# Moving the low part of weight sum S1 behind the next turn's first partial sum

## The chip, the cores and the metric

One core of a Trainium2 chip runs the kernel. The metric is device time in microseconds for one execution. TensorE multiplies matrices into PSUM, VectorE (DVE), ScalarE (ACT) and GpSimd (POOL) work on tiles, and SyncE (SP) issues most of the transfers.

## The reference

The kernel computes a two-layer encoder in fp32: 1024 features, 1280 tokens (1024 of one sequence, 256 of another). Each layer has a mixer of three kinds of heads and then a SwiGLU feed-forward part; the change is in the latter:

```
hf = rmsnorm(x, g_pre_ffn)
f = (jax.nn.silu(hf @ w_gate) * (hf @ w_up)) @ w_down
return x + rmsnorm(f, g_post_ffn)
```

`w_gate` and `w_up` have 2816 columns, which is 22 blocks of 128.

## The kernel before

Everything is written out by hand: one instruction list per engine, and semaphores between them. Each engine works through its own list in order.

**Splitting.** For fp32 accuracy each operand is split in a high part (ScalarE copies it to the fp32r type) and a low part (the operand minus its high part, formed by VectorE or GpSimd). A product is then made of high times high, high times low and low times high: three matmuls where there would be one.

**Turns.** Gate and up are computed together with a Strassen-like scheme: seven products instead of eight, over sums of weight blocks (S1 to S4) and sums of stream blocks (T1 to T4). One *turn* is the seven products for one block of 128 columns and one half of the tokens, in this order: A11, S2, A12, S3, S1, A22, S4. A product is 4 x 3 matmuls. A turn of token half 0 is wide (384 columns), one of half 1 narrow (256 columns). There are 44 turns per layer, numbered t = 0 to 43. A *visit* is one block of weights: visits 0 to 8 have one wide turn each (t = 0 to 8), visits 9 to 21 a wide and a narrow one (t = 9 to 34), visits 22 to 30 one narrow one (t = 35 to 43). Weights of the visits alternate between two buffers GR (raw), GH (high) and GL (low), numbered v % 2.

**Within a turn VectorE** forms six partial sums from PSUM (`partial`): u2 after product S2, u3 after S3, gate2 after S1, gate1 after A22, up2 and hid1 after S4. Product S3 reuses the PSUM bank of S2 and waits for u2; A22 waits for u3; S4 waits for gate2. Between them, in the first turn of a visit, VectorE prepares the next visit's weights: the sums S1 and S3 behind u2, S2 behind u3, S4 behind gate2 (`weight_sum`, one line of 128 x 512 each), and the low parts of S2, S3 and S1 (`weight_sum_low`). From visit 2 on, S1 is held in a PSUM bank of its own (`Y_BANK`), and the S1 sum of a visit waits until the S1 low part of the visit before it has been formed:

```
if v > 1:
    dve.wait_ge(s_wlo_v, 3 * VISIT[L, v] - 3)
```

**ScalarE** makes the high parts of the sums, in the order S1, raw (three blocks at once), S3, S2, S4. **GpSimd** waits for the raw high part and forms three raw low parts (A22, A11, A12, line 1265), then the S4 low part (1273), and then multiplies `hidden2` (1281), which waits for up2. In turns 8 and 9 it also forms low parts of the stream for token half 1 (line 1288: B11, B21, then T1, T4, B22), which products of turn 10 read first; VectorE forms T2 and T3 (line 2035) at the start and the end of turn 9. In turns 3 and 5 GpSimd has a `fold` (line 1244) ahead of its raw low parts.

**The last turns.** Behind turns 38, 40 and 42 VectorE forms the sum S3B (line 2109) and the low part DWL (line 2169) for the down product, and behind turns 39, 41 and 43 the low part DHL (line 2180).

Of the kernel before, what the change touches and what calls it, by code (L numbers as in the profile page):

```python
# [75 lines left out]
NV = len(VISITS)  # L76
TURNS = [(v, u, g) for v, (u, gs) in enumerate(VISITS) for g in gs]
# [375 lines left out]
def build(nc, xt, w_in, w_out, w_gu, w_down, gains, conv_w, rpb, tables, small, mixed,  # L453
          parked, hidden, out):
    with ExitStack() as ctx:
# [315 lines left out]
        def product_at(L, t, name):  # L771
            return NPR * (TURN[L, t] - 1) + PRODUCTS.index(name) + 1

        def turns_of(f):
            return [t for t, (_, u, _) in enumerate(TURNS) if u == f]

        def stored(L, t):
            return 32 * (NT // 2 * L + t // 2 + 1)
# [69 lines left out]
        def summed_weights(L, v, name):  # L848
            return 4 * (VISIT[L, v] - 1) + SUM_ORDER.index(name) + 1

        def high_weights(L, v, name):
            return 5 * (VISIT[L, v] - 1) + HIGH_ORDER[v].index(name) + 1

        def weight_sum_at(v, name):

            if name == "S1" and v > 1:
                return PS[:, Y_BANK, :].rearrange("p (t n) -> p t n", n=P)
            if name == "S2" and v >= EVENTS_OVER:
                return PS[:, SUM_BANK, :].rearrange("p (t n) -> p t n", n=P)
            return GR[v % 2][:, BLOCK[name], :, :]  # L860
# [4 lines left out]
        def bank(t, which):  # L865
            return 3 * (t % 2) + "abc".index(which)
# [1086 lines left out]
        def _(dve):  # L1953
# [63 lines left out]
            def mix(L, g, name):  # L2017

                key, C = (L, g, name), CF[g]
                if name == "T1":  # L2020
                    dve.wait_ge(s_xn, XNORM[L, 2 * g + 1, KT - 1])
                    if g == 0:
                        dve.wait_ge(s_group, GROUP[L, "o", 5, 3])
                else:
                    dve.wait_ge(s_mixsum, MIXSUM[key] - 1)
                out, a, b = {"T1": ("T1", "T3", "B11"), "T2": ("T2", "B22", "T1"), "T3": ("T3", "B22", "T3"),
                             "T4": ("T4", "B21", "T2")}[name]
                nc.vector.tensor_tensor(C[out][:, :, :], C[a][:, :, :], C[b][:, :, :], ALU.subtract) \
                    .then_inc(s_mixsum, MIXSUM.step(key))

            def combination_low(L, g, name):

                dve.wait_ge(s_chi, CHI[L, g, name])
                dve.wait_ge(s_mixsum, MIXSUM[L, g, AFTER[name]])
                nc.vector.tensor_tensor(CL[g][name][:, :, :], CF[g][name][:, :, :], CH[g][name][:, :, :].bitcast(F32),
                                        ALU.subtract).then_inc(s_clo_v, CLO_V.step((L, g, name)))
# [28 lines left out]
            def weight_sum_low(L, v, name):  # L2065

                m = BLOCK[name]
                dve.wait_ge(s_whi, high_weights(L, v, name))
                dve.wait_ge(s_wsum, summed_weights(L, v, "S4" if name == "S2" else "S2" if name == "S1" else "S3"))
                nc.vector.tensor_tensor(GL[v % 2][:, m, :, :], weight_sum_at(v, name),  # L2070
                                        GH[v % 2][:, m, :, :].bitcast(F32), ALU.subtract).then_inc(s_wlo_v, 1)

            def partial(L, t, what):

                n, key = widths[TURNS[t][2]], TURN[L, t]
                T1, U2, U3 = (tile[t % 2][:, 0:n] for tile in (S1T, U2T, U3T))
                a, b, c = (PS[:, bank(t, which), 0:n] for which in "abc")
                if what == "u2":
                    dve.wait_ge(s_product, product_at(L, t, "S2"))
                    dve.wait_ge(s_first, key)  # L2080
                    if key > 2:
                        dve.wait_ge(s_hout[t % 2], stored(L, t) - 32)
                    nc.vector.tensor_tensor(U2, b, T1, ALU.add).then_inc(s_u2, 1)  # L2083
                elif what == "u3":
                    dve.wait_ge(s_product, product_at(L, t, "S3"))
                    if key > 2:
                        dve.wait_ge(s_hid2, key - 2)
                    nc.vector.tensor_tensor(U3, b, T1, ALU.add).then_inc(s_u3, 1)
                elif what == "gate2":
                    dve.wait_ge(s_product, product_at(L, t, "S1"))  # L2090
                    dve.wait_ge(s_u3, key)
                    nc.vector.tensor_tensor(U3, c, U3, ALU.add).then_inc(s_gate2, 1)
                elif what == "gate1":
                    dve.wait_ge(s_product, product_at(L, t, "A22"))
                    nc.vector.tensor_tensor(T1, b, T1, ALU.add).then_inc(s_gate1, 1)
                elif what == "up2":
                    dve.wait_ge(s_product, product_at(L, t, "S4"))
                    dve.wait_ge(s_u2, key)
                    nc.vector.tensor_tensor(U2, c, U2, ALU.add).then_inc(s_up2, 1)
                else:  # L2100
                    dve.wait_ge(s_silu1, key)
                    nc.vector.tensor_tensor(T1, a, T1, ALU.mult).then_inc(s_hid1, 1)

            def sum_s3(L, p):

                n = AT_STEP["A11", p]
                dve.wait_ge(s_s3in, 16 * NPAIR * (L + 1))
                dve.wait_ge(s_ring_w[n % RING], ring_loads(L, n)[0])
                nc.vector.tensor_tensor(S3B[p][:, :, :], DWR[n % RING][:, :, :], S3B[p][:, :, :], ALU.subtract) \
                    .then_inc(s_s3, 1)  # L2110
# [331 lines left out]
            for L in range(DEPTH):  # L2442
# [97 lines left out]
                for t, (v, _, g) in enumerate(TURNS):  # L2540
                    prepare = (t == 0 or TURNS[t - 1][0] != v) and v + 1 < NV
                    partial(L, t, "u2")
                    if t == 0:
                        combination_low(L, 0, "T1")
                        combination_low(L, 0, "T4")
                    if t == 8:
                        mix(L, 1, "T4")
                        mix(L, 1, "T3")
                    if t == 9:
                        combination_low(L, 1, "T2")  # L2550
                    if prepare and v:
                        weight_sum(L, v + 1, "S1")
                        weight_sum(L, v + 1, "S3")
                    if 1 <= t < 5:
                        for k in range(2):
                            step(e, 2 + t // 3, 4 - 4 * (t % 2) + k)
                    if t in (5, 7):
                        for k in range(3) if t == 5 else range(5, KT):
                            normed(L, 2 + t // 7, k)
                    partial(L, t, "u3")  # L2560
                    if t == 0:
                        combination_low(L, 0, "B22")
                    if prepare and v:
                        weight_sum(L, v + 1, "S2")
                    partial(L, t, "gate2")
                    if prepare and v:
                        weight_sum(L, v + 1, "S4")
                    if prepare:
                        weight_sum_low(L, v + 1, "S2")
                    partial(L, t, "gate1")  # L2570
                    if prepare:
                        weight_sum_low(L, v + 1, "S3")
                        weight_sum_low(L, v + 1, "S1")
                    partial(L, t, "up2")
                    partial(L, t, "hid1")
                    if 1 <= t < 5:
                        for k in range(2, 4):
                            step(e, 2 + t // 3, 4 - 4 * (t % 2) + k)
                    if t in (5, 6):
                        for k in range(3, KT) if t == 5 else range(5):  # L2580
                            normed(L, t - 3, k)
                    if t == 7:
                        for name in MIX_ORDER[:2]:
                            mix(L, 1, name)
                    if t == 9:
                        combination_low(L, 1, "T3")
                    if t in EARLY_AT:
                        sum_s3(L, EARLY_AT.index(t))
                        down_low_weights(L, EARLY_AT.index(t))
                    if t - 1 in EARLY_AT:  # L2590
                        down_low_stream(L, EARLY_AT.index(t - 1))
# [539 lines left out]
```

## Time and profile before

| | us |
|---|---|
| median of 3 runs | 3009.96 (3009.44 to 3010.25) |
| the profiled execution, its own time | 3009.93 |
| its span in the profile | 3008.1 |
| TensorE busy | 2977.9 (99%) |
| VectorE busy | 2017.8 (67%) |
| ScalarE busy | 1240.6 (41%) |
| GpSimd busy | 928.9 (31%) |

A busy share is an average over all stages. TensorE's is so near to the span that other engines matter only where TensorE waits for them, so the places to look at are single gaps of tenths of a microsecond. Matmuls overlap in the profile (each is shown longer than the distance to the next), so a short gap shows in the distance between starts.

### The profile page before, as it was taken

What the parts mean: (1) busy time and instruction counts of PE and PEld (TensorE: products, weight loads), DVE (VectorE), ACT (ScalarE), POOL (GpSimd) and SP (SyncE); (2) the same over time, 40 slices, a digit from 0 to 9 for tenths busy, and PEclk for the clock granted to TensorE, in tenths of its full rate; (3) what the DMA queues carried; (4) which work ended last, traced back from release to release, by engine and by line L of the source; (5) the groups of instructions that cost most, each with busy time, mean ns of one, the idle gap of its engine ahead of it and who ended that gap; (6) DMA issues with size and microseconds to landing.
All of it is one profiled execution on the core that took longest, in us unless ns stands there. A gap on an engine that the chain in (4) does not pass through costs nothing.

```text
span 3008.1 us, 50968 instructions
## 1 busy us (share of the span) xinstructions
PE 2977.9 (99%) x19620; PEld 2819.5 (94%) x19620; DVE 2017.8 (67%) x3735; ACT 1240.6 (41%) x2401; POOL 928.9 (31%) x762
## 2 busy tenths in 40 slices
PE   9999999999999999999999999999999999999998
PEld 8888888999999999999988888889999999999998
DVE  7866766388744447677888667573886444486786
ACT  5433444544422225444554344444543222254342
POOL 1211111665532225101442111127555222360013
PEclk9999999999999999999999999999999999999999
DMA  4111011333222226644531110122332222257345
GB/s 157 45 58 52 22 39 57 116 106 110 95 69 72 69 70 198 211 140 152 180 108 47 50 57 20 41 66 100 120 116 93 71 69 69 81 177 253 98 141 197
DMA packets 151568, 300.32 MB, mean 100 GB/s; under 512 B 16288, under 2 KB 74272, under 8 KB 151072
## 3 DMA queue, kind: packets, MB, share of 16 engines
q1 hardware_dynamic: 148336, 288.00, 28.8%
q10 hardware_dynamic: 2992, 9.05, 0.8%
q8 instruction: 159, 2.61, 0.4%
q14 instruction: 81, 0.66, 0.1%
HBM read 231.45 MB, written 57.67 MB: 96 GB/s over the span
## 4 chain that ended last, share of the span: by engine, by line
PE 91%; DVE 4%; POOL 1%; issue 1%; ACT 1%; DMA 1%; SPq 0%; POOLq 0%; DVEq 0%; ACTq 0%
PE PS L2663 27%; PE PS L2665 26%; PE PS L2664 26%; PE PS L2784 4%; PE PS L2815 3%; PE PS L2799 3%; PE PS L2701 1%; POOL OSS L1237 1%; PE PS L2759 1%; DVE ACCUM L1986 0%; PE PS L2824 0%; DVE PT L2383 0%; DMA ACCUM<-xt 0%; DVE SW L2274 0%; DMA DHR<-hidden 0%
## 5 line engine op out<-in xcount | busy, mean ns | idle before, releaser
L2663 PE MATMUL PS<-XH,WH 128*128 128x512 f32 (+1 forms) x1152 | 432.0, 375 | 4.2 <-DVE XL L2230 1.7
L2665 PE MATMUL PS<-XH,WL 128*128 128x512 f32 (+1 forms) x1152 | 409.6, 356 | 0.0
L2664 PE MATMUL PS<-XL,WH 128*128 128x512 f32 (+1 forms) x1152 | 407.9, 354 | 0.0
L1265 POOL TENSOR_TENSOR GL<-GR,GH 128x512 fp32r<-128x512 f32 x186 | 251.8, 1365 | 366.5 <-ACT GH L1614 304.8
L2663 PE MATMUL PS<-DHH,DWH 128*128 128x384 f32 (+1 forms) x1056 | 328.5, 311 | 1.1 <-DVE ACCUM L2215 1.1
L2665 PE MATMUL PS<-DHH,DWL 128*128 128x384 f32 (+1 forms) x1056 | 326.6, 309 | 0.0
L2664 PE MATMUL PS<-DHL,DWH 128*128 128x384 f32 (+1 forms) x1056 | 325.9, 309 | 0.0
L2663 PEld LDWEIGHTS PS<-XH,WH 128*128 128x128 f32 x1152 | 217.2, 189 | 53.3 <-issue 17.7
L2665 PEld LDWEIGHTS PS<-XH,WL 128*128 128x128 f32 x1152 | 217.2, 189 | 32.9
L2664 PEld LDWEIGHTS PS<-XL,WH 128*128 128x128 f32 x1152 | 217.9, 189 | 24.6
L2664 PE MATMUL PS<-CL0T,GH 128*128 128x384 f32 x704 | 238.4, 339 | 0.0
L2663 PE MATMUL PS<-CH0T,GH 128*128 128x384 f32 x704 | 237.7, 338 | 0.0
L2665 PE MATMUL PS<-CH0T,GL 128*128 128x384 f32 x704 | 236.2, 335 | 0.0
L1571 ACT ACTIVATE PT<-PS 128x512 fp32r<-128x512 f32 (+1 forms) x328 | 142.8, 477 | 223.9 <-PE PS L2799 219.6
L1319 POOL COPY RC<-STAT 128x128 f32<-128x128 f32 x100 | 31.9, 319 | 633.6 <-DVE STAT L2392 633.3
L2663 PE MATMUL PS<-CH1T,GH 128*128 128x256 f32 x704 | 198.4, 282 | 2.7 <-DVE U2T L2083 2.7
L2663 PEld LDWEIGHTS PS<-DHH,DWH 128*128 128x128 f32 x1056 | 198.9, 188 | 1.5 <-DVE ACCUM L2215 1.3
L2665 PEld LDWEIGHTS PS<-DHH,DWL 128*128 128x128 f32 x1056 | 198.7, 188 | 0.0
L2664 PEld LDWEIGHTS PS<-DHL,DWH 128*128 128x128 f32 x1056 | 198.6, 188 | 0.0
L2665 PE MATMUL PS<-CH1T,GL 128*128 128x256 f32 x704 | 198.4, 282 | 0.0
L2664 PE MATMUL PS<-CL1T,GH 128*128 128x256 f32 x704 | 196.8, 279 | 0.0
L2383 DVE TENSOR_TENSOR PT<-PS,PT 128x512 fp32r<-128x512 f32 (+1 forms) x328 | 163.8, 531 | 32.5 <-ACT PT L1571 31.0
(242 smaller groups left out, 8341.3 us busy)
## 6 DMA issues: line engine op xcount, KB each, us to landing
GR<-w_gu SPq DMA_DIRECT2D x62, 768.0 KB, 4.2
RAW<-w_in SPq DMA_DIRECT2D x48, 512.0 KB, 3.5
DHR<-hidden SPq DMA_DIRECT2D x66, 320.0 KB, 4.7
DWR<-w_down SPq DMA_DIRECT2D x66, 256.0 KB, 4.0
S3B<-w_down SPq DMA_DIRECT2D x66, 256.0 KB, 3.3
GR<-w_gu SPq DMA_DIRECT2D x62, 256.0 KB, 2.5
T3B<-hidden SPq DMA_DIRECT2D x44, 320.0 KB, 4.0
hidden<-S1T SPq DMA_DIRECT2D x44, 192.0 KB, 1.9
```

The source lines that it names most:

```text
L1237: nc.gpsimd.tensor_tensor(into, into, pair_of(e, kind, c)[:, k % 2, 0:n], ALU.add) \
L1265: nc.gpsimd.tensor_tensor(GL[v % 2][:, m, :, :], GR[v % 2][:, m, :, :], GH[v % 2][:, m, :, :].bitcast(F32), ALU.subtract).then_inc(s_wlo_r ...
L1319: nc.gpsimd.tensor_copy(RC[:, :, :], SM[:, a:a + 2].unsqueeze(2).to_broadcast([P, 2, HD])) \
L1571: nc.scalar.activation(PT[u % 2][:, 0, a:a + n, :].rearrange("p t q -> p (t q)"), PS[:, 4 + g, 0:n * P], ACT.Copy).then_inc(s_pth, 1)
L2383: nc.vector.tensor_tensor(PT[u % 2][:, 1, a:a + n, :].rearrange("p t q -> p (t q)"), PS[:, 4 + g, 0:n * P], high.bitcast(F32), ALU.subtract) \
L2663: nc.tensor.matmul(out, wh, xh, start=first, stop=False, skip_group_check=reopened)
L2664: nc.tensor.matmul(out, wh, xl, start=False, stop=False, skip_group_check=reopened)
L2665: return nc.tensor.matmul(out, wl, xh, start=False, stop=last, skip_group_check=reopened)
L2701: last = nc.tensor.matmul(PS[:, at, j:j + 1], sq[:, j * P:(j + 1) * P], ones[:, 0:1], start=m == 0, stop=m == len(squares) - 1)
L2784: last = nc.tensor.matmul(PS[:, 2 * h + a // 4, 0:n * P], qs[own, :], k[own, keys], start=m == 0, stop=m == 2)
L2799: last = nc.tensor.transpose(PS[:, 4 + g, j * P:(j + 1) * P], PR[:, u % 2, (a + j) * P:(a + j + 1) * P], ident)
L2815: last = nc.tensor.matmul(PS[:, Y_BANK, 2 * P * h:2 * P * h + 2 * P], values_of(b, i, k0, a, h), PT[h][:, :, a, :], start=a == 0, stop=a = ...
```

## The change

In the list of VectorE the S1 low part of the next visit leaves its place behind the S3 low part, ahead of up2. It is formed in the following turn, right behind u2 and ahead of everything else in that turn. The wait of the S1 sum quoted above stays, and the instruction on which it waits now stands right in front of it where the next turn forms sums. No other engine's list changes.

```diff
                 for t, (v, _, g) in enumerate(TURNS):
                     prepare = (t == 0 or TURNS[t - 1][0] != v) and v + 1 < NV
                     partial(L, t, "u2")
+                    if t and (t == 1 or TURNS[t - 2][0] != TURNS[t - 1][0]) and TURNS[t - 1][0] + 1 < NV:
+                        weight_sum_low(L, TURNS[t - 1][0] + 1, "S1")
                     if t == 0:
                         combination_low(L, 0, "T1")
                         combination_low(L, 0, "T4")
...
                     partial(L, t, "gate1")
                     if prepare:
                         weight_sum_low(L, v + 1, "S3")
-                        weight_sum_low(L, v + 1, "S1")
                     partial(L, t, "up2")
                     partial(L, t, "hid1")
```

VectorE's list at the end of turn 40 and the start of turn 41, before. `GL<-GR,GH` is the S3 low part, `GL<-PS,GH` behind it the S1 low part, `U2T<-PS,U2T` up2, `S1T<-PS,S1T` hid1, `S3B` and `DWL` the early work of the down product, `U2T<-PS,S1T` u2 of turn 41 and `PS<-GR` the S1 sum.

```order
 L2070 TENSOR_TENSOR GL_203<-GR_205,GH_201 128x512
 L2070 TENSOR_TENSOR GL_203<-PS,GH_201 128x512
 L2099 TENSOR_TENSOR U2T_155<-PS,U2T_155 128x256
 L2102 TENSOR_TENSOR S1T_153<-PS,S1T_153 128x256
 L2109 TENSOR_TENSOR S3B_268<-DWR_218,S3B_268 128x512
 L2169 TENSOR_TENSOR DWL_213<-DWR_218,DWH_208 128x512
 L2083 TENSOR_TENSOR U2T_156<-PS,S1T_154 128x256
 L2063 TENSOR_TENSOR PS<-GR_206 128x512
```

The same place after the change.

```order
 L2070 TENSOR_TENSOR GL_203<-GR_205,GH_201 128x512
 L2099 TENSOR_TENSOR U2T_155<-PS,U2T_155 128x256
 L2102 TENSOR_TENSOR S1T_153<-PS,S1T_153 128x256
 L2109 TENSOR_TENSOR S3B_268<-DWR_218,S3B_268 128x512
 L2169 TENSOR_TENSOR DWL_213<-DWR_218,DWH_208 128x512
 L2083 TENSOR_TENSOR U2T_156<-PS,S1T_154 128x256
 L2070 TENSOR_TENSOR GL_203<-PS,GH_201 128x512
 L2063 TENSOR_TENSOR PS<-GR_206 128x512
```

The S1 low part has moved from ahead of up2 to between u2 and the S1 sum of the next turn.

VectorE's list at the start of turn 8, as a piece of the difference. `CF1T` are the mixes of the stream.

```order
 L2028 TENSOR_TENSOR CF1T_171<-CF1B_168,CF1T_170 128x1024
 L2083 TENSOR_TENSOR U2T_155<-PS,S1T_153 128x384
+L2070 TENSOR_TENSOR GL_203<-PS,GH_201 128x512
 L2028 TENSOR_TENSOR CF1T_172<-CF1B_167,CF1T_171 128x1024
 L2028 TENSOR_TENSOR CF1T_169<-CF1B_168,CF1T_169 128x1024
```

Here the low part stands ahead of two mixes, which are followed by the S1 sum of turn 8.

## Rows read from the trace of the kernel before

**Rows 1.** Both turn stretches summed (676:1216, 2167:2710): busy us of each engine.
```profile
sum 1083.00, PE 1080.33 PEld 1078.36 DVE 649.10 ACT 377.45 POOL 449.86; mean PE 540.16 PEld 539.18 DVE 324.55 ACT 188.72 POOL 224.93
```
**Rows 2.** Timeline, VectorE, turns 39 to 41: start, us, line, out<-in, idle before.
```profile
1182.78 1.35 DVE L2180 TENSOR_TENSOR DHL<-DHR,DHH 128x640 fp32r<-128x640 f32 x1
1184.06 0.41 DVE L2083 TENSOR_TENSOR U2T<-PS,S1T 128x256 f32<-128x256 f32 x1
1184.39 0.68 DVE L2063 TENSOR_TENSOR PS<-GR 128x512 f32<-128x512 f32 x1
...
1189.86 1.65 DVE L2070 TENSOR_TENSOR GL<-GR,GH 128x512 fp32r<-128x512 f32 x1
1191.43 0.68 DVE L2070 TENSOR_TENSOR GL<-PS,GH 128x512 fp32r<-128x512 f32 x1
...
1192.37 0.41 DVE L2102 TENSOR_TENSOR S1T<-PS,S1T 128x256 f32<-128x256 f32 x1
1192.70 1.22 DVE L2109 TENSOR_TENSOR S3B<-DWR,S3B 128x512 f32<-128x512 f32 x1
1194.02 0.69 DVE L2169 TENSOR_TENSOR DWL<-DWR,DWH 128x512 fp32r<-128x512 f32 x1
1194.63 0.42 DVE L2083 TENSOR_TENSOR U2T<-PS,S1T 128x256 f32<-128x256 f32 x1
```
**Rows 3.** Timeline, TensorE, end of product A12 and start of S3, turn 41.
```profile
1194.44 0.28 PE L2664 MATMUL PS<-CL1B,GH 128*128 128x256 f32 x1
1194.56 0.28 PE L2665 MATMUL PS<-CH1B,GL 128*128 128x256 f32 x1
1195.19 0.36 PE L2663 MATMUL PS<-CH1T,GH 128*128 128x256 f32 x1 [0.35 <-DVE U2T L2083]
```
**Rows 4.** Timeline, GpSimd, turn 40.
```profile
1187.16 3.80 POOL L1265 TENSOR_TENSOR GL<-GR,GH 128x512 fp32r<-128x512 f32 x3 [3.71 <-ACT GH L1614]
1190.92 1.75 POOL L1273 TENSOR_TENSOR GL<-GR,GH 128x512 fp32r<-128x512 f32 x1
1192.63 0.73 POOL L1281 TENSOR_TENSOR U2T<-U2T,U3T 128x256 f32<-128x256 f32 x1
```
**Rows 5.** Timeline, ScalarE, turn 40: the raw high part.
```profile
1185.60 1.48 ACT L1614 ACTIVATE GH<-GR 128x1536 fp32r<-128x1536 f32 x1
```
**Rows 6.** One line's instructions: duration ns min/median/max of low parts that read PSUM.
```profile
L2070 DVE TENSOR_TENSOR GL<-PS,GH x102: 676/678/694, 702.3 to 2703.5; 128x512 fp32r<-128x512 f32 x102
```
**Rows 7.** Timeline, VectorE, turn 9.
```profile
814.51 1.92 DVE L2035 TENSOR_TENSOR CL1T<-CF1T,CH1T 128x1024 fp32r<-128x1024 f32 x1
816.34 1.51 DVE L2063 TENSOR_TENSOR PS<-GR 128x512 f32<-128x512 f32 x1
...
825.75 3.13 DVE L2035 TENSOR_TENSOR CL1T<-CF1T,CH1T 128x1024 fp32r<-128x1024 f32 x1
```
**Rows 8.** Timeline, GpSimd, turns 8 to 10.
```profile
805.10 3.81 POOL L1265 TENSOR_TENSOR GL<-GR,GH 128x512 fp32r<-128x512 f32 x3 [7.89 <-ACT GH L1614]
...
810.58 4.76 POOL L1288 TENSOR_TENSOR CL1B<-CF1B,CH1B 128x1024 fp32r<-128x1024 f32 x2
815.30 2.00 POOL L1281 TENSOR_TENSOR U2T<-U2T,U3T 128x384 f32<-128x384 f32 x1
819.94 3.81 POOL L1265 TENSOR_TENSOR GL<-GR,GH 128x512 fp32r<-128x512 f32 x3 [2.64 <-ACT GH L1614]
...
825.40 5.72 POOL L1288 TENSOR_TENSOR CL1T<-CF1T,CH1T 128x1024 fp32r<-128x1024 f32 x2
831.08 2.40 POOL L1288 TENSOR_TENSOR CL1B<-CF1B,CH1B 128x1024 fp32r<-128x1024 f32 x1
```
**Rows 9.** Timeline, TensorE, first matmul of product S4 in turn 10.
```profile
833.68 0.30 PE L2663 MATMUL PS<-CH1B,GH 128*128 128x256 f32 x1
```
**Rows 10.** Timeline, GpSimd, turn 3: the fold.
```profile
722.10 2.41 POOL L1244 TENSOR_TENSOR MX<-MX 128x1024 f32<-128x1024 f32 x1 [2.89 <-ACT MX L1510]
```
**Rows 11.** Timeline, VectorE, turn 3: the S1 sum.
```profile
722.22 2.83 DVE L2063 TENSOR_TENSOR PS<-GR 128x512 f32<-128x512 f32 x1
```

## The prediction

> **What bounds the kernel now.** I read the stages first: in the two stretches that hold the SwiGLU turns (676 to 1216 us and 2167 to 2710 us) TensorE is busy for 1080.33 of 1083.00 us at the full clock, so it idles 2.7 us in both layers together [rows 1]. That is nearly all that taking work off VectorE's way to TensorE can give there. Then I went through TensorE's instructions by start time for gaps. A product is 12 matmuls that start 0.12 us apart in a narrow turn (1194.44, 1194.56), so about 1.42 us. The reader is to see the gap from 1194.56 to 1195.19: product S3 of turn 41 starts 0.51 us late, released by VectorE's u2 [rows 3]. The same gap stands in turn 43, about the same in turn 10, and in layer 1 again; turn 39 is at its limit. Last I read VectorE, GpSimd and ScalarE side by side ahead of these gaps [rows 2, 4, 5].
>
> What they show is a hand-over. A VectorE instruction with both inputs in SBUF does not run while a GpSimd instruction does. In turn 40 the S3 low part is issued at 1189.86 and takes 1.65 us, not 0.69, ending 0.55 us after GpSimd's three raw low parts do (1187.16 + 3.80 = 1190.96). GpSimd's S4 low part, queued behind them, waits in turn for VectorE and ends at 1192.67 [rows 2, 4]. So whichever of the two waits when the other ends goes next. The low part that is moved reads PSUM and takes 676 to 694 ns in all 102 cases, beside GpSimd or not [rows 6].
>
> The Trainium skill says the same (SBUF — State Buffer, "Who interferes with whom"): the port that VectorE and GpSimd share is an exclusive lock, taken by a VectorE instruction with two SBUF inputs and not by one that reads PSUM; the rows above agree. A reader who knew only the durations, without the lock, would count the edit at zero or a gain of a few tenths in each late turn.
>
> **What the change removes and adds.** No instruction is added or removed, no DMA moves. In each visit one VectorE instruction of 0.68 us leaves the place between the S3 low part and up2, and comes back behind u2 of the next turn. Leaving costs nothing and frees 0.60 us (1191.43 to up2, whose successor hid1 starts 0.34 us later, at 1192.37). Coming back costs where a first weight sum S1 stands behind u2, which is in turns 1 to 9 and 36 to 42. In turns 11 to 35 it either comes back in the second turn of a visit, where VectorE has no sums to form, or not at all: zero. The product S1 needs the moved low part only two products after u2 (over 2.8 us), so it never waits for it.
>
> *Size of the shift.* Today the S1 sum starts 0.33 us after u2 (1184.06, 1184.39). After the change it starts behind 0.33 + 0.68 us of low part, and also waits for that low part's semaphore, since it overwrites the PSUM bank that this reads. A wait on VectorE's own last result costs about 0.10 us (the sum S3B ends at 1193.92, DWL starts at 1194.02) [rows 2]. So S1 starts 1.11 us after u2: a shift of 0.78 us. Behind S1 are queued S3, u3, the other sums; and ScalarE's high part of S1, then its raw high part (1185.60, ends 1187.08), which releases GpSimd's three raw low parts (1187.16) [rows 4, 5]. All of these move by 0.78 us. u3 can stand it: it waits for TensorE anyway, and A22 needs it a product later.
>
> *Turns 38, 40 and 42, which carry the early work of the down product.* GpSimd's raw low parts end 0.78 us later, so the S3 low part, which waits for them, does too. The 0.60 us freed behind it are spent: hid1 ends about 0.2 us later than today. Today the order is then S4 low part (ends E = 1192.67), hidden2 (ends 1193.36), sum of S3B (ends 1193.92, 0.56 behind), DWL, and u2 at 1194.63 = E + 1.96 [rows 2, 4]. Now S3B is issued 0.59 us behind the end of the S3 low part, and E comes 1.16 us behind it (1191.51 to 1192.67). Without the 0.60 us of low part between, S3B is waiting when the S4 low part ends, and goes first: S3B ends at E' + 0.55, hidden2 at E' + 1.23, DWL is blocked by it and ends at E' + 1.78, u2 starts at E' + 1.70. With E' = E + 0.78 that is 0.52 us later than today. These u2 already set the start of product S3, so each 0.52 us is lost by TensorE. Three turns: 1.56 us per layer.
>
> *Turns 39 and 41*, with one DHL of 1.35 us instead: today it waits for hidden2, now it goes ahead of it. That saves 0.71 us (E + 1.31 becomes E' + 0.60) against 0.78 us of shift: 0.07 us on the way to the next late u2, 0.14 us per layer. Sum for the end of a layer 1.70 us, together 3.4 us.
>
> *Turns 8 to 10.* In turn 8 the low part comes ahead of the mixes and pushes the S1 sum by 0.60 us. From there GpSimd has a chain without a gap: raw low parts 805.10, S4 low part, B11 and B21 low parts 810.58 to 815.34. In turn 9 VectorE's T2 low part (814.51, 1.92 us) waits for that end, hidden2 (815.30, 2.00 us) waits for T2, the S1 sum (816.34, 1.51 us) waits for hidden2, and behind it come the raw low parts of turn 9 (819.94), T1 and T4 (825.40, with VectorE's T3 in between) and B22, ending at 831.08 + 2.40 = 833.48 [rows 7, 8]. Product S4 of turn 10, which reads B22, starts at 833.68 [rows 9]. A release takes 0.14 us (u2 of turn 41 ends 1195.05, S3 starts 1195.19), so 0.06 us is free. In turn 9 the low part itself adds nothing, since T2 behind it waits for GpSimd anyway. So 0.60 - 0.06 = 0.54 us per layer, 1.1 us. The gap that u2 leaves in turn 10 today may close (T3 may go ahead of T1), but TensorE then waits at S4 instead: the end is the same.
>
> *Turns 1 to 7*: in turns 3 and 5 the S1 sum waits for GpSimd's fold (722.10, 2.41 us; the sum takes 2.83 us), so the low part fits under that wait [rows 10, 11]. In 1, 2, 4, 6 and 7 products are 384 columns wide instead of 256 and give VectorE longer cover than the narrow ones, where the moved part alone costs nothing. Zero; if that cover were missing, up to 0.78 us in each.
>
> Sum: 3.4 + 1.1 = **4.5 us**. The profiled execution took 3009.93 us (span 3008.1), next to the median of 3009.96, so 3014.4 us.
>
> **Rivals.**
> *The shift does not reach GpSimd's end* (the S1 sum's delay is taken up before the raw low parts). Then the 0.60 us before up2 is a gain: the late u2 of turns 41, 43 and 10 come up to 0.60 us earlier, and the gaps close. Its most is the idle time of [rows 1], 2.7 us, and at the outside 4 us counting what lies in start gaps alone: 3006 to 3007.3 us. For it: these gaps are real. Against: the raw low parts start 0.08 us after ScalarE's raw high part ends, with no slack. It decides if the raw low parts of turn 40 start no later relative to u2.
> *Only part of it shows*: the B22 chain has slack I don't see (then 3.4 us are left), or the later sums in a turn catch up part of the 0.78 us because GpSimd's last two low parts are held by something else. With half of the late turns' term and no B22 chain, 1.7 us remain: 3011 to 3013 us.
> *Today's order stays* (hidden2 ahead of S3B): then u2 keeps its E + 1.96 and each of turns 38, 40 and 42 loses the whole 0.78 us: 4.7 + 1.1 = 5.8 us, 3015.7 us.
> *Dearer own wait.* Nowhere is a wait of this kind in front of S1 to be seen; bounds are 0.03 us (nothing but the end of the low part) and 0.5 us. Each 0.1 us above my 0.10 adds 0.6 us over six late turns; and above a shift of about 0.75 us GpSimd's second raw low part (1187.16 + 2.54 = 1189.70) comes late for the product A11 of turn 41, which starts three products ahead of S3's due time, 1194.68 - 4.26 = 1190.42. At 0.5 us: 4.5 + 2.4 = 6.9 us, 3016.8 us, which would be measurably slower.
> *The change does nothing*: all shifts covered, 3010 us.
>
> **How the numbers follow.** I give the forecast (3013 to 3015.5) 0.48, part of it 0.15, today's order 0.07, the dearer wait 0.12, nothing 0.07, the gain 0.11. About 0.2%, or 6 us, is what can be told from no change. Slower by more than that needs the dearer wait, or today's order with every turn lost: 0.17 (0.12 and most of 0.07). Faster by more would need over 6 us where only some 4 us of gaps stand: 0.03. The range runs from 3007.3, the near end of the gain, to 3016.8, the dear wait.
>
> **What the profile after would show.** u2 of turn 41 stands about 0.6 us further behind u2 of turn 39 than today, S3B stands ahead of hidden2 behind the S4 low part, and TensorE's gap ahead of product S3 in turns 39, 41 and 43 is near 0.5, 1.1 and 1.1 us. In turn 10 the gap is ahead of S4 with B22 as what it waits for, in part or whole. TensorE's idle time in the two stretches rises from 2.7 to about 7 us. I am wrong if GpSimd's raw low parts don't move against u2, or if gaps show up in turns 11 to 35.

## The result, and the profile after

| | before | after |
|---|---|---|
| median | 3009.47 us (3006.11 to 3013.76, 21 runs) | 3012.91 us (3010.85 to 3016.73, 21 runs) |
| ratio, 95% interval | | 1.0015 [1.0009, 1.0021], which is 4.5 us slower (2.7 to 6.3) |
| turns of layer 0 / layer 1 | 549.62 / 549.78 us | 551.70 / 551.81 us |

The last line is the time from the first matmul of turn 0 to the last of turn 43, from the starts of matmuls in the profiled executions. Its sum over both layers grows by 4.1 us; the two medians lie 3.4 us apart, and the ratio gives 4.5 us. Single executions differ by some microseconds in stages that the change does not touch, so this line tells more than the spans do (3008.1 and 3010.5 us).

Windows of after: both turn stretches, the busy time of each engine. The windows are 6 us longer than in [rows 1], so that they still cover the same turns.

```profile
sum 1089.00, PE 1084.02 PEld 1080.86 DVE 650.80 ACT 375.08 POOL 454.20; mean PE 542.01 PEld 540.43 DVE 325.40 ACT 187.54 POOL 227.10
```

TensorE idles 4.98 us where it idled 2.67. This view undercounts a gap: a matmul is shown for 0.28 us where the next could start 0.12 us later, so 0.16 us of every gap passes as busy. Starts of matmuls give the whole gap.

Timeline of VectorE in after, turns 39 to 41.

```profile
1182.52 1.25 DVE L2180 TENSOR_TENSOR DHL<-DHR,DHH 128x640 fp32r<-128x640 f32 x1
1183.69 0.41 DVE L2083 TENSOR_TENSOR U2T<-PS,S1T 128x256 f32<-128x256 f32 x1
1184.03 0.67 DVE L2070 TENSOR_TENSOR GL<-PS,GH 128x512 fp32r<-128x512 f32 x1
1184.80 0.70 DVE L2063 TENSOR_TENSOR PS<-GR 128x512 f32<-128x512 f32 x1
...
1190.28 1.66 DVE L2070 TENSOR_TENSOR GL<-GR,GH 128x512 fp32r<-128x512 f32 x1
1191.86 0.41 DVE L2099 TENSOR_TENSOR U2T<-PS,U2T 128x256 f32<-128x256 f32 x1
1192.19 0.41 DVE L2102 TENSOR_TENSOR S1T<-PS,S1T 128x256 f32<-128x256 f32 x1
1192.53 1.12 DVE L2109 TENSOR_TENSOR S3B<-DWR,S3B 128x512 f32<-128x512 f32 x1
1193.75 1.04 DVE L2169 TENSOR_TENSOR DWL<-DWR,DWH 128x512 fp32r<-128x512 f32 x1
1194.71 0.41 DVE L2083 TENSOR_TENSOR U2T<-PS,S1T 128x256 f32<-128x256 f32 x1
```

Read it against [rows 2]. The S1 sum starts 1.11 us behind u2 of turn 40 (1183.69, 1184.80); it was 0.33. From u2 of turn 40 to u2 of turn 41 is 11.02 us; it was 10.57. Timelines of ScalarE and GpSimd in after, turn 40:

```profile
1186.03 1.48 ACT L1614 ACTIVATE GH<-GR 128x1536 fp32r<-128x1536 f32 x1
```
```profile
1187.59 3.80 POOL L1265 TENSOR_TENSOR GL<-GR,GH 128x512 fp32r<-128x512 f32 x3 [3.22 <-ACT GH L1614]
1191.35 1.74 POOL L1273 TENSOR_TENSOR GL<-GR,GH 128x512 fp32r<-128x512 f32 x1
1193.06 1.18 POOL L1281 TENSOR_TENSOR U2T<-U2T,U3T 128x256 f32<-128x256 f32 x1
```

The raw low parts start 3.90 us behind u2 (1183.69, 1187.59), where they started 3.10 us behind it [rows 2, 4]: the shift arrives whole. The S4 low part ends at 1193.09 (1191.35 + 1.74). S3B, issued at 1192.53, ends 0.56 us behind that, and `hidden2`, which took 0.73 us before [rows 4], now takes 1.18 us, because now it waits for S3B. Then DWL waits for `hidden2`: 1.04 us instead of 0.69.

TensorE in after: the last matmul ahead of product A11 of turn 40 and its first one, then the same for S3 of turn 41.

```profile
1179.92 0.28 PE L2666 MATMUL PS<-CH1B,GL 128*128 128x256 f32 x1
1180.29 0.36 PE L2664 MATMUL PS<-CH1B,GH 128*128 128x256 f32 x1
...
1194.48 0.28 PE L2666 MATMUL PS<-CH1B,GL 128*128 128x256 f32 x1
1195.27 0.36 PE L2664 MATMUL PS<-CH1T,GH 128*128 128x256 f32 x1 [0.51 <-DVE U2T L2083]
```

S3 of turn 41 starts 0.67 us late (0.79 less 0.12). There is also a gap that was not there before: the first matmul of A11 comes 0.37 us behind the one ahead of it, so 0.25 us late. Every such break costs some 0.08 us more at the next matmul (it starts 0.19 to 0.20 us behind the late one, not 0.12). 0.25 + 0.67 + 2 x 0.08 = 1.08 us for the pair of turns 40 and 41. In turn 10 the waits have moved too. TensorE in after, the last matmul ahead of A22 and its first, then the same for S4:

```profile
829.82 0.28 PE L2666 MATMUL PS<-CH1T,GL 128*128 128x256 f32 x1
830.39 0.36 PE L2664 MATMUL PS<-CH1T,GH 128*128 128x256 f32 x1 [0.29 <-POOL CL1T L1288]
...
831.77 0.28 PE L2666 MATMUL PS<-CH1T,GL 128*128 128x256 f32 x1
832.74 0.36 PE L2664 MATMUL PS<-CH1B,GH 128*128 128x256 f32 x1 [0.69 <-POOL CL1B L1288]
```

These are the waits of TensorE for other engines in layer 0's turns (who waits <- for what: us, times, longest); the gaps ahead of A11 are too short for this view.

```profile
PE PS L2664 <- DVE U2T L2083: 1.3, 3, 0.5
PE PS L2664 <- POOL CL1B L1288: 0.7, 1, 0.7
PE PS L2664 <- POOL CL1T L1288: 0.3, 1, 0.3
```

### The profile page after: what moved, and what is told of

Read it like the earlier page. It is cut to its first block, busy times and chain, and to the rows that moved or that the text cites. A ratio compares the mean times of both kernels' runs of the same rounds, so it can differ in the third digit from the quotient of the medians.

```text
span 3010.5 us, 50968 instructions
## 1 busy us (share of the span) xinstructions
PE 2976.6 (99%) x19620; PEld 2817.3 (94%) x19620; DVE 2020.0 (67%) x3735; ACT 1239.4 (41%) x2401; POOL 933.1 (31%) x762
## 4 chain that ended last, share of the span: by engine, by line
PE 89%; DVE 4%; POOL 2%; issue 2%; ACT 1%; DMA 1%; SPq 0%; DVEq 0%; POOLq 0%; ACTq 0%
PE PS L2664 26%; PE PS L2666 25%; PE PS L2665 25%; PE PS L2785 4%; PE PS L2816 3%; PE PS L2800 3%; PE PS L2702 1%; POOL OSS L1237 1%; PE PS L2760 1%; ACT GH L1621 0%; DMA DHR<-hidden 0%; POOL CL1T L1288 0%; DVE ACCUM L1986 0%; ACT GH L1614 0%; PE PS L2825 0%
```

## The experiments

One measure serves all: in each layer, the time from the first matmul of turn 0 to the first of S4 of turn 10 (the early part), and from there to the last matmul of turn 43 (the late part). Values are layer 0 / layer 1, from starts of matmuls, in one profiled execution of each kernel; the median and the ratio are of the whole program. The kernel before was run again beside each; its medians went from 3009.09 to 3010.34 us, so the ratios are to be compared and not the medians.

| kernel | early part | late part | median us | ratio to before |
|---|---|---|---|---|
| before | 161.94 / 161.94 | 387.68 / 387.84 | | |
| after | 162.47 / 162.59 | 389.23 / 389.22 | 3012.91 | 1.0015 [1.0009, 1.0021] |
| late turns only | 161.98 / 161.99 | 389.12 / 389.16 | 3011.81 | 1.0008 [0.9998, 1.0017] |
| turns 1 to 9 only | 162.51 / 162.54 | 387.61 / 387.63 | 3009.93 | 1.0001 [0.9991, 1.0010] |
| middle turns only | 161.96 / 161.95 | 387.93 / 387.68 | 3009.93 | 1.0001 [0.9991, 1.0011] |
| turn 8 only | 162.60 / 162.56 | 387.95 / 387.70 | 3008.05 | one run |
| turns 1 to 9 without 8 | 161.94 / 161.94 | 387.65 / 387.65 | 3009.35 | one run |
| behind hid1 | 162.44 / 162.44 | 387.64 / 387.64 | 3009.73 | 1.0001 [0.9992, 1.0010] |
| behind hid1, not turn 7 | 162.02 / 162.01 | 387.63 / 387.66 | 3013.6 | one run |
| low part twice | 162.52 / 162.52 | 393.77 / 393.76 | 3024.56 | 1.0045 [1.0032, 1.0059] |
| work moved | 161.70 / 161.72 | 386.35 / 386.34 | 3007.13 | 0.9989 [0.9980, 0.9998] |
| T4 on VectorE | 162.62 / 162.62 | 386.34 / 386.34 | 3008.15 | 0.9995 [0.9986, 1.0004] |
| T4 and B22 on VectorE | 161.15 / 161.15 | 386.42 / 386.45 | 3004.31 | 0.9983 [0.9974, 0.9992] |

**Where the time goes.** Three kernels make the change in one stretch of turns each and leave the low part in its old place in the others (`t > 35` for the first; `t < 10` and `9 < t < 36` for the others, with the matching condition at the old place):

```diff
                     partial(L, t, "u2")
-                    if t and (t == 1 or ...) and TURNS[t - 1][0] + 1 < NV:
+                    if t and (t == 1 or ...) and TURNS[t - 1][0] + 1 < NV and t > 35:
                         weight_sum_low(L, TURNS[t - 1][0] + 1, "S1")
...
                         weight_sum_low(L, v + 1, "S3")
+                        if t < 35:
+                            weight_sum_low(L, v + 1, "S1")
```

> The S1 low part is moved in turns 36 to 43 only; everywhere else it stands as before. My theory (the low part ahead of the S1 sum delays ScalarE's and GpSimd's chain, and the early down work then waits for it): TensorE's turn stretch, from the first product of turn 0 to product S3 of turn 43, is 1.5 to 1.7 us longer per layer than before, all of it from turn 39 on; product S4 of turn 10 stays at its place (158.3 us after the start). Time +3.1 us, 3012.6 us. Rival (every turn that takes the low part in pays some of its 0.68 us, the middle ones too): clearly less than the 4.1 us of the whole change, as only 8 of 29 moves per layer are made, about 1.1 us.

> The S1 low part is moved in turns 1 to 9 only. My theory: GpSimd's chain from turn 8 to B22 ends about 0.6 us later, product S4 of turn 10 stands 0.5 to 0.6 us later per layer than before (158.9 instead of 158.3 us after the start of the stretch) and nothing else changes: time +1.1 us, 3010.6 us. Rival (the loss in turn 10 comes from the low part of visit 10 that is formed in turn 10, or from T3 that trades places with T1): no shift here, or one that ends before S4.

> The S1 low part is moved only where it comes back in turns 10 to 34, of which only the second turns of a visit take one in. My theory: none of these has an S1 sum behind it, so nothing waits; the one thing that can change is turn 10, where T3 is issued 0.6 us sooner and may go ahead of T1, with product S4 at the same place or up to 0.1 us off. Time +0.0 us, 3009.5 us. Rival (each turn that takes it in pays): 14 moves per layer, some us in both layers together, gaps on TensorE in turns 11 to 34.

The late turns alone cost 1.44 and 1.32 us in the late part and nothing in the early part; turns 1 to 9 alone cost 0.57 and 0.60 us in the early part and nothing in the late one; the middle turns cost nothing: the 0.25 us by which their layer 0 is longer (387.93, with 387.68 in the other layer) comes from a late transfer, read further down. The two parts add up: 1.44 + 1.32 + 0.57 + 0.60 = 3.9 us against 4.1 us for the whole change. The ratios alone would not have told this: no interval of the three excludes 1.

**Which of the early turns.** One kernel makes the move only from turn 7 to turn 8 (`t == 8`), the other in turns 1 to 9 but not there.

> Of all moves only one per layer is made: the S1 low part of visit 8 leaves turn 7 and is formed behind u2 of turn 8. My theory (a chain on GpSimd without a gap from turn 8's raw low parts to B22): product S4 of turn 10 is late by the same 0.5 to 0.6 us per layer as with all nine moves of turns 1 to 9 (158.9 where before it is 158.3 from the second matmul, or 162.5 for 161.94 counted from the first), all the rest unchanged, 1.1 us in time. Rival (the nine moves add up): at most 0.1 us.

> The S1 low part is moved in turns 1 to 9 except turn 8. My theory: product S4 of turn 10 at its old place, 161.94 us after the start of the stretch, and the stretch as long as before (549.6 to 549.8 us). Rival (the nine moves add up): 0.4 to 0.5 us later per layer.

Turn 8 has all of it (+0.66, +0.62), the others nothing to the hundredth. But TensorE loses it in another place than in after: in these two kernels (turn 8 only, turns 1 to 9) T3 still goes behind T1 and takes 3.13 us, u2 comes late behind it, and the gap stands ahead of S3 of turn 10. In after, where turn 9 loses its low part too, it stands ahead of A22 and S4. So these runs show that turn 8 delays GpSimd's chain, not that B22 is the end at which the delay counts; that is read from after itself.

**The low part in a third place.** Here it leaves its old place too, so in the late turns up2 and hid1 come 0.6 us earlier, but it stands behind hid1 of its own turn and not in front of the S1 sum.

```diff
                     partial(L, t, "u2")
-                    if t and (t == 1 or ...) and TURNS[t - 1][0] + 1 < NV:
-                        weight_sum_low(L, TURNS[t - 1][0] + 1, "S1")
...
                     partial(L, t, "hid1")
+                    if prepare:
+                        weight_sum_low(L, v + 1, "S1")
```

> The S1 low part leaves its place ahead of up2 in every turn, but comes back behind hid1 of the same turn, ahead of the early down work; the next turn's S1 sum stands right behind u2 as before. My theory (only coming back behind u2 costs; leaving gives nothing because S3B then waits as long for GpSimd): the late turns are as before within 0.1 us each, S4 of turn 10 at its old place, time +0.0 us, 3009.5 us. Rival (leaving the place ahead of up2 is a gain, or costs by turning the order of S3B and hidden2): the gaps ahead of S3 in turns 41 and 43 shrink by up to 0.5 us each, or grow by as much, time 2 us off on either side.

The late part is as before: leaving the place ahead of up2 costs nothing, the new place in front of the sum costs the 1.55 and 1.38 us. (Behind hid1 the low part still stands ahead of S3B, so `hidden2` keeps going first; this kernel says nothing on the other order.) The early part missed its expectation by 0.50 us. Timeline of VectorE in this kernel, end of turn 7, and then of hid1 in the kernel before:

```profile
793.51 0.56 DVE L2099 TENSOR_TENSOR U2T<-PS,U2T 128x384 f32<-128x384 f32 x1 [0.53 <-PE PS L2666]
794.86 0.56 DVE L2102 TENSOR_TENSOR S1T<-PS,S1T 128x384 f32<-128x384 f32 x1 [0.79 <-ACT S1T L1659]
795.33 0.68 DVE L2070 TENSOR_TENSOR GL<-PS,GH 128x512 fp32r<-128x512 f32 x1
795.93 1.22 DVE L2028 TENSOR_TENSOR CF1T<-CF1T,CF1B 128x1024 f32<-128x1024 f32 x1
```
```profile
796.49 0.56 DVE L2102 TENSOR_TENSOR S1T<-PS,S1T 128x384 f32<-128x384 f32 x1 [0.78 <-ACT S1T L1659]
```

hid1 waits for ScalarE in this turn, 0.79 us here and 0.78 us before, so it comes no earlier when the low part leaves. The low part was free in its old place: without it up2 waits 0.53 us for TensorE. Behind hid1 it pushes the mixes, and with them u2 and the S1 sum of turn 8. So I kept the old place for turn 7 alone:

```diff
+                    if t == 7:
+                        weight_sum_low(L, v + 1, "S1")
                     partial(L, t, "up2")
                     partial(L, t, "hid1")
-                    if prepare:
+                    if prepare and t != 7:
                         weight_sum_low(L, v + 1, "S1")
```

> The kernel with the S1 low part behind hid1, except in turn 7, where it keeps its place ahead of up2. There the kernel with all of them behind hid1 was 0.5 us late at product S4 of turn 10; my reading is that ahead of hid1 VectorE waits 0.79 us for ScalarE and the low part is free there, behind it it pushes the mixes, u2 and the S1 sum of turn 8. Then S4 of turn 10 is back at 161.94 us and the stretch at 549.6 to 549.8 us per layer. Rival (any low part behind hid1 costs, wherever): still 0.3 to 0.5 us late.

The early part falls back to 162.02, within 0.08 us of before. (Its one time of 3013.6 us comes from stages outside the turns, which take 549.64 and 549.67 us; the mean granted clock of that run was 0.995.)

**Twice the cost in front of the sum.** After, with the low part formed twice in turns 36 to 42, the second waiting for the first.

```diff
+                        if t > 35 and t < 43:
+                            weight_sum_low(L, TURNS[t - 1][0] + 1, "S1", False)
                         weight_sum_low(L, TURNS[t - 1][0] + 1, "S1")
```

> The changed kernel, but in turns 36 to 42 the S1 low part is formed twice behind u2, one behind the other with a wait between, so that the S1 sum is shifted by 1.56 us against before instead of 0.78. My theory (the shift goes whole through ScalarE and GpSimd to u2 of the next turn): u2 of turns 39 to 43 each come 0.78 us later once more; turns 40 and 42 had 0.1 us of slack, so all five lose, about 3.5 to 3.9 us per layer on top of the change. Stretch 9 to 10 us longer than before per layer pair at least: time about +11.5 us, 3021 us. Rival (the loss is a fixed cost of the turned order of S3B and hidden2, not of the shift): no more than 1 us on top of the change.

From S3 of turn 39 to S3 of turn 43 (layer 0) a turn takes 11.07, 11.37, 11.07 and 11.39 us where after takes 10.35, 10.67, 10.35 and 10.69: 0.70 to 0.72 us for each repetition, next to the 0.78 us of the working. In all these turns u2 starts without idle time behind VectorE's own work, so the loss is VectorE's. But the time missed the expectation by some 3 us. The waits of TensorE in layer 0's turns show where the larger part went (lines are one to eight higher in this kernel):

```profile
PE PS L2672 <- POOL GL L1266: 3.0, 7, 0.6
PE PS L2672 <- DVE U2T L2089: 1.5, 3, 0.5
```

Seven waits are for GpSimd's raw low parts, ahead of product A11 of turns 37 to 43. Turns 37 and 38 lose nothing after the single change; once the shift is doubled, the second of the three raw low parts comes 0.40 us too late for their A11, and they take 10.43 and 10.42 us instead of 9.95. That is 1.9 us in both layers together. I had worked the expectation out without it, though it is the threshold that the rival of the dearer wait names. The rest of the 3 us is not in the turns, which grew by 13.2 us against before, and four runs don't settle it.

**Taking the cost away.** The gaps of before stand where u2 is late, and the S1 sum is queued behind u2. If what is queued ahead of these two is what TensorE waits for, the gaps must close when it is taken away. This kernel puts the S1 low part at the end of its turn, S3B, DWL and DHL one turn later behind the S3 sum, and the low part of B22 on VectorE, behind u3 of turn 10. (Against before; lines that only keep the numbering in step are left out.)

```diff
-POOL_LOW = ((), ("B11", "B21", "T1", "T4", "B22"))
+POOL_LOW = ((), ("B11", "B21", "T1", "T4"))
...
                         weight_sum(L, v + 1, "S3")
+                    if t - 1 in EARLY_AT:
+                        sum_s3(L, EARLY_AT.index(t - 1))
+                        down_low_weights(L, EARLY_AT.index(t - 1))
+                    if t - 2 in EARLY_AT:
+                        down_low_stream(L, EARLY_AT.index(t - 2))
...
                     partial(L, t, "u3")
+                    if t == 10:
+                        combination_low(L, 1, "B22")
...
-                    if t in EARLY_AT:
-                        sum_s3(L, EARLY_AT.index(t))
-                        down_low_weights(L, EARLY_AT.index(t))
-                    if t - 1 in EARLY_AT:
-                        down_low_stream(L, EARLY_AT.index(t - 1))
+                    if prepare:
+                        weight_sum_low(L, v + 1, "S1")
...
```

> The kernel before with three places changed, each meant to clear one thing that TensorE waits for: the S1 low part at the end of its turn, the early down work (S3B, DWL, DHL) out of the way of u2, behind the S3 sum of the next turn, and the low part of B22 on VectorE in turn 10 instead of last in GpSimd's chain. If u2 in turns 41 and 43 and B22 in turn 10 are what TensorE waits for, all those gaps go: 0.75 us in turn 10 and 0.5 to 0.6 in turns 41 and 43, some 1.8 to 2.0 us per layer, time -3.8 us, 3005.7 us. If GpSimd's chain holds turn 10 anyway at T4, 0.1 to 0.7 us of that stays; if u3 comes late because of the work ahead of it, TensorE waits at A22 instead and the time is as before.

The late part falls by 1.33 and 1.50 us against before and has no gap left. The early part still loses 0.55 us against the last kernel of this section: A22 of turn 10 waits for T4 at the end of GpSimd's chain. The next kernel gives T4 to VectorE, behind u2 of turn 10, leaves B22 on GpSimd, and keeps turn 7's S1 low part in its old place.

```diff
+POOL_LOW = ((), ("B11", "B21", "T1", "B22"))
+VECTOR_LOW = (("B11", "T2", "B21", "T3", "T1", "T4", "B22"), ("T2", "T3", "T4"))
...
                     partial(L, t, "u2")
+                    if t == 10:
+                        combination_low(L, 1, "T4")
...
```

> The kernel with the moved work, but of the stream's low parts for turn 10 VectorE forms T4 right behind u2 (instead of B22 behind u3), GpSimd forms T1 and then B22, and in turn 7 the S1 low part keeps its old place ahead of up2, where VectorE waits for ScalarE anyway. If T4 at the end of GpSimd's chain is what was left of the wait in turn 10, the last 0.55 us per layer go: product S4 of turn 10 at 161.2 us after the start of the stretch instead of 161.7, the stretch 547.5 us instead of 548.05, time -4.4 us against before, 3005.4 us. If GpSimd's chain as a whole is too long, it stays at 548.0 us and -3.3 us.

The early part got worse: 162.62. Timelines of GpSimd and of VectorE in this kernel, end of turn 9:

```profile
823.92 2.39 POOL L1288 TENSOR_TENSOR CL1T<-CF1T,CH1T 128x1024 fp32r<-128x1024 f32 x1
```
```profile
823.95 3.44 DVE L2035 TENSOR_TENSOR CL1T<-CF1T,CH1T 128x1024 fp32r<-128x1024 f32 x1
827.31 0.68 DVE L2070 TENSOR_TENSOR GL<-PS,GH 128x512 fp32r<-128x512 f32 x1
827.91 0.41 DVE L2083 TENSOR_TENSOR U2T<-PS,S1T 128x256 f32<-128x256 f32 x1
```

GpSimd's T1 starts 0.03 us ahead of VectorE's T3, so T3 waits out all of T1 and takes 3.44 us, and u2, behind it and the S1 low part, makes product S3 late by 1.37 us (0.16 us of it under a matmul that the row still shows as running). I had expected 0.5 us less than with the moved work, and it is 0.9 us more. The last kernel takes both T4 and B22 off GpSimd (T4 behind u2, B22 behind u3) and puts the S1 low part at the end of all turns as in the kernel before it.

```diff
+POOL_LOW = ((), ("B11", "B21", "T1"))
+VECTOR_LOW = (("B11", "T2", "B21", "T3", "T1", "T4", "B22"), ("T2", "T3", "T4", "B22"))
```

> The kernel with the moved work, S1 low part of turn 7 behind hid1 again (so that T3 is issued before GpSimd's T1 and goes first), and both T4 and B22 formed by VectorE in turn 10, behind u2 and behind u3; GpSimd forms only T1 there. My theory: T3 takes 1.4 us as in the kernel with the moved work, and not the 3.4 us it took where GpSimd was 0.03 us ahead; T1 then ends in time, and TensorE waits for nothing in turn 10: product S4 at 161.1 to 161.3 us after the start of the stretch (161.7 with the moved work, 162.6 where T1 went first), stretch 547.5 us, time -4.4 us against before, 3005 us. Rival (VectorE has no room for two low parts in turn 10): TensorE waits at A22 or S4 for u3 or gate2, the stretch 548 us or more, -3.3 us or less.

Timeline of VectorE in this kernel, turns 9 and 10 (T3, T4, B22), then a window over the turns of layer 0 (busy us and count of TensorE, its loads, VectorE, ScalarE, GpSimd; granted clock; DMA):

```profile
824.16 1.38 DVE L2035 TENSOR_TENSOR CL1T<-CF1T,CH1T 128x1024 fp32r<-128x1024 f32 x1
...
826.40 2.49 DVE L2035 TENSOR_TENSOR CL1T<-CF1T,CH1T 128x1024 fp32r<-128x1024 f32 x1
...
829.14 1.70 DVE L2035 TENSOR_TENSOR CL1B<-CF1B,CH1B 128x1024 fp32r<-128x1024 f32 x1
```
```profile
672.00:1220.00 548.00, 548.00 (x3752) 547.56 (x3751) 328.80 (x540) 191.40 (x313) 222.43 (x172) 1.00 0.29 97
```

T3 goes ahead of T1 and takes 1.38 us, and TensorE is busy for 548.00 of 548.00 us. The turns take 547.57 and 547.60 us, 4.2 us less than before in both layers together; the ratio makes the whole program 5 us faster (2.4 to 7.8), and the medians are 3004.31 and 3010.34 us. It is the fastest version, and it sets the floor of the turns from which the losses below are counted.

## Why the prediction was right

**The shift of the S1 sum**, worked out as 0.78 us, is 0.78 us (1.11 less 0.33), and the wait for VectorE's own last result is 0.10 us of it: the low part ends at 1184.70, the sum starts at 1184.80. It arrives at GpSimd whole, as 0.80 us. The rival of a dearer wait falls as far as the price goes, and so does the rival in which the shift doesn't reach GpSimd's end.

**Turns 38, 40 and 42.** S3B goes ahead of `hidden2` and DWL waits, in the order worked out. u2 of turn 41 starts 1.62 us behind the end of the S4 low part (1193.09, 1194.71), worked out as 1.70; so today's order did not stay. The 0.08 us lie in `hidden2`, which ends 1.15 us behind the S4 low part (1193.09, 1194.24) where I had 1.23. u2 of turn 41 stands 0.45 us further behind u2 of turn 40 than before, where I had 0.52.

**The size.** Product S3 of turns 39, 41 and 43 lost 0.44, 0.52 and 0.53 us more than before in layer 0, counted from S3 of turn 34, where I had 0.52, 0.59 and 0.59. Each turn with S3B costs 0.45 us instead of 0.52; a turn with DHL costs the 0.07 us of the working (from u2 of turn 39 to u2 of turn 40 it is 10.00 us, and was 9.93). That is 1.49 us instead of 1.70. The measured late part, 1.55 us, also holds the 0.07 us that the second matmul of S4 loses behind the new gap of turn 10. In layer 1 it is 1.38 us, because turn 39 there was already 0.18 us late in before (see the end of this section). So the sum had 0.5 us too much for the late turns and 0.1 too little for the early ones: 4.5 us, and the turns grew by 4.1.

The median of 3012.91 us by itself would not have told this. It lies just below the 3013 to 3015.5 us to which I gave the largest chance, in what I gave to "only part of it shows", and before ran 0.5 us faster here than the 3009.96 us from which I counted. An interval of 2.7 to 6.3 us cannot tell 4.5 us from the 5.8 us of the rival with today's order either; the order read above does.

**Turns 8 to 10** cost 0.53 and 0.65 us, worked out as 0.54, and the move into turn 8 alone costs as much. Timeline of VectorE in after, turn 9, T3:

```profile
824.26 1.38 DVE L2035 TENSOR_TENSOR CL1T<-CF1T,CH1T 128x1024 fp32r<-128x1024 f32 x1
```

T3 now goes ahead of T1 (1.38 us, against 3.13 in [rows 7]), the gap that u2 left in turn 10 is gone, and TensorE waits for GpSimd instead, for T4 ahead of A22 and for B22 ahead of S4: as foreseen, but for T4. Against the fastest version the early part of before had lost 0.79 us to u2, and that of after 1.32 us to GpSimd. GpSimd's chain in after is as gapless as in [rows 8]:

```profile
804.23 3.81 POOL L1265 TENSOR_TENSOR GL<-GR,GH 128x512 fp32r<-128x512 f32 x3 [8.50 <-ACT GH L1614]
...
809.71 4.75 POOL L1288 TENSOR_TENSOR CL1B<-CF1B,CH1B 128x1024 fp32r<-128x1024 f32 x2
...
824.51 5.73 POOL L1288 TENSOR_TENSOR CL1T<-CF1T,CH1T 128x1024 fp32r<-128x1024 f32 x2
830.21 2.39 POOL L1288 TENSOR_TENSOR CL1B<-CF1B,CH1B 128x1024 fp32r<-128x1024 f32 x1
```

**Turns 1 to 7 and 11 to 35** cost nothing, as worked out; the kernels without turn 8 and with the middle turns alone show it.

**What the profile should have shown and did not.** I gave gaps of 0.5, 1.1 and 1.1 us ahead of S3. They are 0.43, 0.67 and 0.67 us. The loss per pair of turns is near what I gave (0.52 us against 0.59), but part of it stands ahead of A11 of turns 40 and 42 (0.25 us each), where GpSimd's second raw low part comes late. The prediction has this limit, at a shift of 0.75 us, but for A11 of turn 41 alone; in turns 39 and 41 u2 is later against TensorE than in turn 40, and the limit is passed sooner. That gap adds nothing here, because u2 of turns 40 and 42 starts right behind DHL, on VectorE's own account. I also gave 7 us of idle time; the window shows 4.98, because each new gap lies partly under a matmul's shown duration. The idle time was an error in how the check was put; the gap ahead of A11 was overlooked, and it would have cost something if u2 had not been late anyway.

**The same shift without the change.** The late part is 387.84 us in layer 1 of before and 387.93 us in layer 0 of the kernel with the middle turns, where the other late parts without the shift are 387.61 to 387.70 us, but for one named below. Timelines of VectorE, u2 and S1 sum of turn 38, in the first and then in the second:

```profile
2654.96 0.42 DVE L2083 TENSOR_TENSOR U2T<-PS,S1T 128x256 f32<-128x256 f32 x1 [1.22 <-PE PS L2665]
2655.47 0.70 DVE L2063 TENSOR_TENSOR PS<-GR 128x512 f32<-128x512 f32 x1
```
```profile
1162.38 0.42 DVE L2083 TENSOR_TENSOR U2T<-PS,S1T 128x256 f32<-128x256 f32 x1 [1.21 <-PE PS L2668]
1162.98 0.70 DVE L2063 TENSOR_TENSOR PS<-GR 128x512 f32<-128x512 f32 x1 [0.17 <-DMA GR<-w_gu]
```

The S1 sum waits for the transfer of its raw weights (in the first for 0.09 us, too short for the row to mark) and starts 0.51 and 0.60 us behind u2 instead of 0.34. S3 of turn 39 is then 0.18 and 0.24 us late: the whole shift, with no instruction moved, and with `hidden2` still ahead of S3B. So a shift costs its full length while today's order stays, and of the 0.79 us that reach the S4 low part of turn 40 in after (its end is 9.40 us behind u2 and was 8.61) the other order gives back 0.34: u2 of turn 41 is 0.45 us later.

The shift is shown as the cause: with the low part behind hid1, and no shift, the late part is as before; with twice of it every turn from 39 to 43 takes another 0.70 to 0.72 us; and late transfers that shift the same sum cost what they shift it by. The kernels with moved work change several things at once and show only that the gaps of before come from what stands ahead of u2. Not settled is a gap of 0.22 us ahead of A12 of turn 11 in one layer of one kernel (turn 8 only, 387.95), for which the profile names no releaser.

## What to carry to other kernels

Moving a short instruction off an engine's late stretch gains only if its new place is not ahead of the first link of the chain that makes the next stretch late; look for what is queued behind the new place, on that engine and on the engines it releases. Where an engine fills the span to 99%, count the starts of its instructions between two fixed points of the program: 0.05 us can be read there, once a late transfer like that of turn 38 (0.2 us) is told apart, while the time of the program moves by several us from run to run. And move a step into a place where its engine waits for something else anyway, as the low part did ahead of up2 of turn 7, which otherwise waits for TensorE; the same step two instructions later cost 0.5 us.

## What the runs showed of the hardware

Between VectorE and GpSimd, 0.03 us of issue order decided 2 us: T3 took 1.38 us where it was issued first and 3.44 us where it came 0.03 us behind T1. In the cases read here the one that waits goes next when the other ends, even when the other has its next instruction queued: the S3 low part takes 1.66 us and the S4 low part behind it 1.74 us in after, and `hidden2` grows from 0.73 to 1.18 us and DWL from 0.69 to 1.04 us once S3B goes ahead of them. An instruction that waited ends less than its full time behind the end of the other: S3B 0.56 us, where one of 128x512 that does not wait takes 0.69, and T3 1.08 us (827.39, 826.31), where it takes 1.38 unhindered. The low part that reads PSUM was held up by none of this in after either; one line's instructions (ns: shortest, median, longest):

```profile
L2070 DVE TENSOR_TENSOR GL<-PS,GH x102: 674/682/693, 706.1 to 2710.6; 128x512 fp32r<-128x512 f32 x102
```

The Trainium skill says (SBUF — State Buffer, "Who interferes with whom") that a VectorE instruction with two SBUF inputs contends with GpSimd for a shared port, that one with at most one such input, outside some faster modes, does not, and that the order of issue decides who is blocked; these runs agree, with the numbers above.
